# Splitting each head's first weights one unit earlier, opening the projection on half the tokens, and reordering the last gathers

## The reference

```python
def mixer(h, ...):                      # h = rms_norm(x, norm_mix_g), D_MODEL = 1024
    proj = h @ w_in
    aq, ak, av, hq, hff, hfb, hi, hg = jnp.split(proj, ...)
    att = diff_attention(...)           # 4 heads; softmax(q k) - lam * softmax(q' k'), with a distance bias
    o_f, o_b = hgrn2_chunk_scan(...)    # 4 heads; a gated linear scan forwards and backwards, chunks of 64
    return jnp.concatenate([att, hgo], axis=-1) @ w_out

def trunk(x, ...):
    x = x + mixer(rms_norm(x, norm_mix_g), ...)
    h = rms_norm(x, norm_ffn_g)
    x = x + expert_choice_ffn(h, ...)   # 16 experts, each takes its top tokens (64 of the prompt, 128 of the sample)
    return rms_norm(x, final_norm_g)
```

## Time and profile before

| what | value |
| --- | --- |
| runs | 2251.47, 2244.16, 2246.93 us |
| median | 2246.93 us |
| profiled execution, its own time | 2244.6 us |
| its span, first to last instruction | 2242.8 us |
| mean granted TensorE clock | 0.958 |
| PE busy | 2024.3 us, 90% |
| DVE busy | 1470.4 us, 66% |
| ACT busy | 1110.6 us, 50% |

### The profile page before, as it was taken

How to read it: one execution, slowest core, us unless ns; L and a number is a source line. 1 busy time by engine, 2 the same in 40 slices (tenths; PEclk the granted TensorE clock), 3 DMA queues, 4 the chain that set the end, 5 groups by cost and what they waited for, 6 DMA issues and landing times. The chain is left out here.

```text
span 2242.8 us, 43810 instructions
## 1 busy us (share of the span) xinstructions
PE 2024.3 (90%) x16048; PEld 1763.0 (79%) x16048; DVE 1470.4 (66%) x2769; ACT 1110.6 (50%) x1983; POOL 299.2 (13%) x419
## 2 busy tenths in 40 slices
PE   6999998899897899778799649999999999999996
PEld 5777776677776677667688549999999999999995
DVE  4376575666665567656527857777777777778885
ACT  4322222356555532256422236666666666667773
POOL 2001101000000011100122101111111111111234
PEclk9999999999998999979999869999999999999998
DMA  5211110100002121121233157777878788878995
GB/s 168 84 31 31 32 33 16 33 25 19 23 5 75 37 62 56 48 76 47 85 123 113 66 189 238 250 255 251 259 250 258 250 258 249 258 257 311 341 320 184
DMA packets 183451, 317.64 MB, mean 142 GB/s; under 512 B 11872, under 2 KB 82016, under 8 KB 183328
## 3 DMA queue, kind: packets, MB, share of 16 engines
q1 hardware_dynamic: 170560, 283.16, 37.6%
q0 software_dynamic: 8608, 30.68, 5.5%
q10 hardware_dynamic: 4160, 2.10, 0.3%
HBM read 279.97 MB, written 35.91 MB: 141 GB/s over the span
## 5 line engine op out<-in xcount | busy, mean ns | idle before, releaser
L2211 DVE TENSOR_TENSOR we_lo<-raw,we_hi 128x1024 fp32r<-128x1024 f32 x384 | 465.6, 1222 | 190.2 <-ACT we_hi L2136 189.2
L2102 PE MATMUL psum<-x_parts,we_hi 128*128 128x384 f32 x2048 | 586.1, 360 | 3.1 <-DVE we_lo L2211 3.1
L2104 PE MATMUL psum<-x_parts,we_lo 128*128 128x192 f32 x2048 | 513.8, 251 | 0.0
L2136 ACT CAST we_hi<-raw 128x1024 fp32r<-128x1024 f32 x384 | 400.3, 1054 | 157.8 <-PE psum L2104 93.9
L2104 PEld LDWEIGHTS psum<-x_parts,we_lo 128*128 128x128 f32 x2048 | 392.6, 192 | 0.6
L2102 PEld LDWEIGHTS psum<-x_parts,we_hi 128*128 128x128 f32 x2048 | 385.7, 188 | 4.1 <-issue 3.5
L586 PE MATMUL psum<-hT_hi,w_hi 128*128 128x512 f32 x512 | 215.9, 422 | 12.5 <-DVE w_lo L566 12.5
L588 PE MATMUL psum<-hT_hi,w_lo 128*128 128x512 f32 x512 | 203.2, 397 | 0.0
L587 PE MATMUL psum<-hT_lo,w_hi 128*128 128x512 f32 x512 | 202.7, 396 | 0.0
L586 PE MATMUL psum<-hP_hi,w_hi 128*128 128x512 f32 x256 | 111.1, 434 | 22.7 <-DVE w_lo L566 22.7
L586 PEld LDWEIGHTS psum<-hT_hi,w_hi 128*128 128x128 f32 x512 | 97.6, 191 | 34.6 <-DVE land L1099 7.5
(11 more groups left out here) (312 smaller groups left out, 3825.0 us busy)
## 6 DMA issues: line engine op xcount, KB each, us to landing
raw<-in_w_gate SPq DMA_DIRECT2D x128, 512.0 KB, 4.8
raw<-in_w_up SPq DMA_DIRECT2D x128, 512.0 KB, 7.3
raw<-in_w_down SPq DMA_DIRECT2D x128, 512.0 KB, 6.0
w_raw<-in_w_in SPq DMA_DIRECT2D x96, 256.0 KB, 2.8
y_rows<-x SPq DMA_DIRECT2D x12, 512.0 KB, 2.6
h_rows<-h SPq DMA_DIRECT2D x12, 512.0 KB, 2.8
y<-y_rows SPq DMA_DIRECT2D x12, 512.0 KB, 8.0
w_raw_s<-in_w_in SPq DMA_DIRECT2D x16, 256.0 KB, 3.1
```

The lines of the kernel that those rows point to most:

```text
L2102: pe.matmul(out[:, 0:2 * SLOTS], w_hi[:, s, at], x_parts[p][:, k, :, :], start=(k == 0), stop=False, skip_group_check=True)
L2104: mm = pe.matmul(out[:, SLOTS:2 * SLOTS], w_lo[:, s, at], x_hi[p][:, k, :], start=False, stop=(k == DT - 1), skip_group_check=True)
L2136: act.copy(w_hi[:, n % PARTS, :], raw[:, s, :]).then_inc(hi.sem, 1)
L2211: dve.tensor_tensor(w_lo[:, n % PARTS, :], raw[:, n % RAW, :], w_hi[:, n % PARTS, :].bitcast(F32), ALU.subtract).then_inc(lo.sem, 1)
```

## The change

**Opening.** In `turning`, scale and turn of tile t stand ahead of the square of tile t + 2. SP loads g right after x0, and the first two weights between x3 and x4. The splits of units 0 and 1 go in among the sample tiles, and so do the four pieces of units 0 and 1 that use block 0 (tiles 0 to 3); a wait for the rows of these four tiles alone goes with them. Block 1 waits for all tiles.

**Heads.** ("split", 0) of the next head stands right after the piece ("unit", last, 0, 0) of the head before, in the loops and in the lists around them. To write this, `heads()` loops over two iterations and writes the third out in full.

**Tail.** `fetch` of the last late expert stands ahead of the powers of the one before and ahead of its put; the last power and put go part by part (sample, then prompt).

```diff
@@ multiply @@
-            if self.rows and first and u == 0 and b == 0:
-                pe.wait_ge(self.rows.sem, self.rows.last(0))
+            if self.rows and first and u == 0:
+                if self.by_block and b == 0:
+                    pe.wait_ge(self.rows.sem, self.rows.at(0, 2 * BC - 1))
+                elif self.by_block or b == 0:
+                    pe.wait_ge(self.rows.sem, self.rows.last(0))
@@ turning @@
     for t in range(NT + pairs - 1):
+        if t < NT:
+            out += [("scale", t), ("turn", t)]
         if t + 2 < NT:
             out.append(("square", t + 2))
-        if t < NT:
-            out += [("scale", t), ("turn", t)]
@@ mix: the opening's list @@
+    at_tile = {("split", 2): [("split", 0)], ("split", 3): [("split", 1)], ("turn", 5): [("unit", 0, 0, 0)],
+               ("turn", 6): [("unit", 0, 0, 1)], ("turn", 7): [("unit", 1, 0, 0)], ("split", 7): [("unit", 1, 0, 1)]}
+    first_tiles = [s for step in turning(T_SAMPLE // P, 2)
+                   for s in [("n", step), *(("h", of) for of in at_tile.get(step, ()))]]
+    begun = [("unit", 0, 1, 0), ("unit", 0, 1, 1), ("split", 2), ("unit", 1, 1, 0), ("unit", 1, 1, 1)]
@@ program @@
-        def heads(body, steps):
-            with eng.Fori(0, HEADS - 1) as i:
-                for step in steps:
-                    body(step, i, i + 1)
+        def heads(body, steps, units, then=None):
+            for lone in (False, True):
+                with ExitStack() as loop:
+                    i = HEADS - 2 if lone else loop.enter_context(eng.Fori(0, HEADS - 2))
+                    for step in steps:
+                        if step != ("split", 0):
+                            body(step, i, i + 1)
+                        if step == ("unit", units - 1, 0, 0):
+                            if not lone:
+                                body(("split", 0), i, i + 2)
+                            elif then:
+                                then(("split", 0), None, 0)
@@ sync @@
             load(sp, 0)
+            load_g(sp)
             load(sp, 1)
             consts.load_ident(sp)
-            load_g(sp)
+            begin, loads = h_s.loads
             for t in range(2, T_SAMPLE // P):
+                if t == BC:
+                    begin(sp)
                 load(sp, t)
@@ late_steps and after the last pair @@
-                        return [(put, 0), (fetch, 2), (put, 1)] + of_items + [(fetch, 3), (put, 2)]
+                        return [(put, 0), (fetch, 2), (put, 1), (fetch, 3)] + of_items + [(put, 2)]
-                power(NT + 2 * LATE - 2)
-                power(NT + 2 * LATE - 1)
-                put(LATE - 1)
+                for part in range(2):
+                    power(in_turn[part - 2])
+                    put(LATE - 1, (part,))
```

More of the change, by code:

```diff
@@ L514, in __init__ @@
     def __init__(self, sem, T, cols, ring, by_dve, banks, w_in, mem, before=None, rows=None):
+        self.by_block = before is None
         self.cols, self.ring, self.mem, self.banks, self.before, self.rows = cols, ring, mem, banks, before, rows
@@ L560, in split_hi @@
         act.wait_ge(arrived.sem, arrived.at(j, 16 * (u // self.ring) + 15))
-        act.wait_ge(self.summed.sem, self.summed.at(j, self.NB * (u - 1) - 1))
+        used = self.NB * (u - 1) - 1
+        if self.by_block and first and u == 2:
+            used += 1
+        act.wait_ge(self.summed.sem, self.summed.at(j, used))
         act.copy(self.mem.w_hi[:, u % 2, :, :], self.mem.w_raw[u % self.ring]).then_inc(self.hi.sem, 1)
@@ L726, in program @@
                 h[0](step, None, 0)
+                if step == ("unit", h_s.proj.units - 1, 0, 0):
+                    h[0](("split", 0), 0, 1)
             else:
@@ L729, in program @@
         for g, (hs, ats) in enumerate(((h_s, a_s), (h_p, a_p))):
-            heads(h[g], hs.stages[1])
+            heads(h[g], hs.stages[1], hs.proj.units, a[g])
             for kind, step in joined[g]:
@@ L733, in program @@
                     h[g](step, HEADS - 1, None)
-                elif kind == "a":
+                elif kind == "a" and step != ("split", 0):
                     a[g](step, None, 0)
-                else:
+                elif kind == "o":
                     tile(step)
-            heads(a[g], ats.stages[1])
+                if kind == "a" and step == ("unit", ats.proj.units - 1, 0, 0):
+                    a[g](("split", 0), 0, 1)
+            heads(a[g], ats.stages[1], ats.proj.units)
             if g == 0:
@@ L746, in program @@
                         h[1](step, None, 0)
+                        if step == ("unit", h_p.proj.units - 1, 0, 0):
+                            h[1](("split", 0), 0, 1)
         for kind, step in ending:
@@ L767, in _ @@
             load, _ = n_p.loads
-            h_s.loads(sp, lambda: [load(sp, t) for t in range(T_PROMPT // P)])
+            loads(sp, lambda: [load(sp, t) for t in range(T_PROMPT // P)])
             a_s.loads(sp)
             u_p.loads(sp)
-            h_p.loads(sp)
+            h_p.loads[1](sp)
             early, late = o.loads
@@ L893, in all_mixed, with begin_loads @@
             eng.wait_ge(after.signals["mixed"].sem, after.signals["mixed"].last(HEADS - 1))
+    def begin_loads(sp):
+        start_signals(sp, proj.raw_in)
+        for u in range(2):
+            proj.load(sp, 0, None, u)
     def loads(sp, behind_ring=None):
-        start_signals(sp, proj.raw_in)
-        for u in range(proj.units):
+        if after:
+            begin_loads(sp)
+        for u in range(2, proj.units):
             if u == proj.ring and behind_ring:
@@ L2338, in fetch, with put @@
                                                 ).then_inc(late_in[f % 2][part], 16)
-                def put(f):
+                def put(f, parts=(0, 1)):
                     column_of = slice(FIRST_LATE + f, FIRST_LATE + f + 1)
@@ L2345, in put @@
                             pool.wait_ge(y_out[s], 16 * (NT // SLOTS_Y))
-                    for part, (rows, to, of) in enumerate(((late_s, out_s, index_cols[:, 1, column_of]),
-                                                           (late_p, out_p, index_cols[0:CAP_PROMPT, 2, column_of]))):
+                    of_parts = ((late_s, out_s, index_cols[:, 1, column_of]), (late_p, out_p, index_cols[0:CAP_PROMPT, 2, column_of]))
+                    for part in parts:
+                        rows, to, of = of_parts[part]
                         if f:
```

19 lines of the change are left out of this document (11 added, 8 removed).

## The result

| | before | changed |
| --- | --- | --- |
| runs beside each other, median | 2249.06 us (4 runs) | 2209.63 us (4 runs) |
| profiled execution | 2244.6 us | 2209.69 us |
| its span | 2242.8 us | 2207.9 us |
| mean granted clock of TensorE | 0.958 | 0.965 |

The ratio is 0.983, 95% interval 0.9804 to 0.9857: 32 to 44 us are gone. The direction was right. The range (2211 to 2234) missed 2209.63, and 24.3 us had been summed where the two traces lie 34.9 apart. All medians and ratios here are of the kernel's fast runs; one run of the last experiment (4154.67 us) was not one and is left out.

A forecast was written before the change was run, and what follows sets the result against it. PE, busy 90% of the span, was taken as the bound, its `w_lo` waits as the target. Terms 6.7 + 6.6 + 1.9 + 2.0 + 4.0 + 3.1 = 24.3 off 2244.6 gave 2220.3, 2222.6 on the median; forecast 2221, range 2211 to 2234.

The forecast's parts named there:

- The terms of the four loops: Gains from PE's waits in the loops: sample HGRN 6.6, sample attention 1.9, prompt HGRN 2.0, prompt attention 4.0 us.
- Sample attention, 1.9: Sample attention loop: earlier scores gain 1.9 us with ACT's table load on the path; 4.1 if the load hid.
- Opening, 6.7: Opening: 24 early matmuls fill PE's pauses, so units 0 and 1 end at 41.9, not 48.61: 6.7 us.
- Rival 2: Opening at half clock throughout: its gain is 1.1 instead of 6.7 us, total 2225.9; chance 12%.
- Tail, 3.1: Tail: the last fetch, right behind put 1, lets DVE start at about 2220.75 instead of 2223.82: 3.1 us.
- Nothing, within 0.2: Tail: last power and put in parts move sample's scatter forward and prompt's back: no net effect, within 0.2 us.
- 2.0 was summed: Prompt HGRN loop: the shared bank is late next, so only `w_lo`'s own 0.65 goes at three entries: 2.0 us.
- 6.3 against 6.6: Sample HGRN loop: an earlier `w_lo` removes 2.2 us at each of three entries or turns: 6.6 us.
- rival 1: Next in the chain is as late: block 1's bank leaves sample HGRN 2.0, others low ends; 13.1 us, 2231.5; chance 14%.
- Rival 3: Loops' jump: code fetch hidden by the `w_lo` wait shows at each kept turn, up to 4.2 us, 2224.5; chance 6%.
- Rival 4: Written-out loop bodies fetched late: 16 stops of 2.64 us, 42.2 in all, slower at 2262.5; chance 4%.
- The footing: Whole kernel: gains subtracted from the profiled 2244.6 us rather than the median 2246.9, 2.3 us apart.

The follow-up runs named there:

- the last experiment: Changed kernel with all quarters unpacked at once, old order of last puts, HGRN loops written out: 2197.90 us, ratio 0.9791; beside it, with loops kept, 2203.10, 0.981.
- an experiment of its own: Kernel before with the third iteration of each head loop written out and nothing else: 2245.40 us, ratio 1.0003 to the kernel before.

## Why the prediction was wrong

**The step that failed: a wait was priced at its idle time.** The terms of the four loops took the gap of PE and stopped there; the clock behind it was put at nothing. In the traces a gap of 2.1 to 2.6 is followed by a stretch in which the same matmuls run at 1.2 GHz: at two places in four traces of four, which cost 1.5 to 1.7 us each time, and at the sample HGRN loop's entries in seven of twelve, 3.0 a kernel; at the prompt HGRN loop's third entry in none of four. Between the two traces compared, the four loops gave 19.9 us where 14.5 had been summed, and 5.5 of the 19.9 is PE's busy time: some 3 of it half clock at the two places, the rest what overlaps less around a wait. Two of its pieces could have been read ahead: at 981.62 the first matmul lasts 0.79 and not 0.49, as at 36.26 in the opening, and the parts on rivals spoke of the clock for the opening alone. Put back one kind at a time, the loops were worth about 13 and 16 us, with 7 of uncertainty each, where 5.9 and 8.6 had been summed.

**Sample attention, 1.9 against 3.8: a wait was read into an order.** The load of ACT's table was put on the path since a row of the kernel before had it waiting 2.13 for DVE. That row was from straight code. At the loop's head the load ran ahead of the wait; the row ahead of it in the order was taken for the wait for the scores and was not. Read with the load off the path, the term would have been 4.1, the bound that was kept. Some 1.3 of the 3.8 comes with the third iteration written out even where the split is late. The fully written-out kernel has the load where the prediction put it, and there the iteration is 2.4 longer. The same reading put the load on the path of the prompt attention's first two iterations, where it did not wait either.

**Opening, 6.7 against 8.35: a term was cancelled without a row.** The earlier first scale and the two added `w_lo` were let cancel. The first scale came 2.6 sooner, 1.9 arrived on PE, and with it put back the 48 matmuls end at 42.2, where the prediction's own working had 41.9. The clock was taken right: the first piece at half, the rest at full. Rival 2 fell.

**Tail, 3.1 against 2.2: right where it looked.** The fetch gave 3.2. "Nothing, within 0.2" for the last power and put in parts was wrong: it costs 1.2, since the prompt's power is the one that waits behind a scatter, and its norm and scatter still follow.

**What held.** At two of the prompt HGRN loop's entries the waits turned to waits for `land`, 1.41 and 1.50, as said; at the first one 1.9 for `mixT` stayed of 2.40. That 2.7 came where 2.0 was summed is luck: half of it, 1.3, is PE's busy time, the half clock behind the second entry above all. In the sample HGRN loop 6.3 against 6.6 is luck too, for the trace compared had none of the half clock that the others show behind these waits. The sample HGRN loop's entry lost its whole wait, the next bank did not show (rival 1 falls), and the waits for `normed` stayed (6.4 us before, 6.7 now). Rival 3, the jump, was real but small: 0.6 to 0.8 of idle time at one turn. Rival 4 fell by an experiment of its own; its one pause of 2.64 without a releaser was not the only one of the kernel before, which has another of 2.57 at 923.29, and both are still there in the changed kernel.

**The range.** The high end of the sum was 31.4, counted from 2244.6. The clock had no place in it outside the opening, so no end of a term could reach what the loops gave (19.9, where the high ends of the four sum to 18.9). The footing had little part in it: 2221 lies 11.4 over the measured 2209.63, and the two traces show 10.6 of that.

**What stays open.** 4.5 us of the difference between the two traces lie in stages that had no term, 4.0 of them in PE's busy time. There half-clock stretches come and go between runs of the same code, so a part of it is chance; whether another part is systematic the runs can't say. Why a gap of 2.1 is followed by half clock in one run and not in the next was not settled either.

## What to carry to other kernels

Price a wait of PE at its idle time plus what runs at half clock behind it, and look for that in the first matmuls after the gap, whose pitch tells it; look in more than one trace, since the one read here had none behind the three waits of the sample HGRN loop. A place in an instruction list is not a place in time: whether an instruction waits is read from a row of the same kind of code, loop head or straight. When the last steps are split for an earlier start, follow the half that then ends last.

## What the hardware showed that was not expected

- At the prompt attention's first entry a wait of 2.5 to 2.6 us left the matmuls behind it at a clock of 0.51 to 0.56 in four traces of four; without the wait it was 1.00 in ten of ten. At the prompt HGRN loop's second entry it was 0.62 to 0.66 behind waits of 2.09 to 2.38, four of four, and 1.00 behind 1.41 to 1.56, ten of ten.
- A loop's jump back showed as a pause of 0.6 to 0.8 us on PE once the wait for `w_lo` was gone, and the sample HGRN loop written out was some 3 us shorter, most of it by half clock that did not come.
- ACT's table load of 1.28 us ran ahead of the wait at a loop's head and behind it in straight code: 78.4 against 80.7 us for the same iteration.
